# Thirty-two row dots moved from one phase to the other, and one product moved from VectorE to ScalarE, in a hybrid conv, attention and expert-retrieval block

## The chip, the cores and the metric

The kernel runs on one core of a Trainium2 chip. The metric is device microseconds per execution of that core. A TensorE matmul multiplies a stationary 128x128 tile by a moving tile; VectorE (DVE), ScalarE (ACT) and GpSimd (POOL) work on tiles of 128 partitions; SyncE (SP), ACT and POOL issue DMAs. Each engine runs its instructions in program order and waits on semaphores.

## The reference

One layer on 512 tokens of width 2048, in float32. The first half (modulated norm, one input projection, a convolution branch, an attention branch, an output projection) is untouched by the change. The second half, which the change touches, is a product-key retrieval over 16384 single-neuron experts: each token picks 8 x 16 = 128 experts, and its result is a gated sum over their rows of U and V.

```python
def peer(h, wq, k1, k2, u, v):
    ...
    experts = e1 * N_KEYS + e2                      # (tokens, 8, 16), 128 per token
    gates = jax.nn.softmax(best, axis=-1)
    def one_block(args):
        xb, eb, gb = args
        a = jnp.einsum("td,thkd->thk", xb, u[eb])   # row dots with U
        act = gb * jax.nn.gelu(a)
        return jnp.einsum("thk,thkd->td", act, v[eb])  # row steps with V
```

## The kernel before

The 512 tokens are split in three. **352 tokens** (TD) go the dense way: for all 16384 experts the activations are made on TensorE in 128 jobs over U, gated by a scattered gate matrix, and multiplied with V in 128 jobs. **128 tokens** (the last ones) and **32 extra tokens** (XT) go the sparse way: for each of their expert slots, GpSimd gathers a row of U or V for every partition by an indirect DMA (128 x 2048 float32), and VectorE multiplies it with the token ("dot", 128 of them; "dot_x" for the extra tokens, 32 of them) or adds it to the result ("v_step", 128 + 32).

**U jobs** (u_job, numbers 0 to 127). Job g needs tile g of U: SP loads it (load_raw, into one of four buffers, when job g-4 has ended), ACT copies it to a rounded tile (hi_raw, issued behind the Gelu of job g-3), VectorE subtracts to get the low part (lo_raw). TensorE then makes 16 x 3 matmuls of 352 columns. ACT applies Gelu and stores 176 KB to DRAM.

**Hots** (from job HOT = 69 on, 44 turns of 8 tokens, up to job 112). Beside the U job of a turn, VectorE builds one-hot tiles for 8 tokens (build_hots): an equality tile for the second key, one for the first key, and the first one times three bfloat16 pieces of the gate. TensorE multiplies them in 24 small matmuls; ACT copies the result (keep_hots) and stores it every fourth turn.

**End of U.** Jobs 113 to 127 have no hots. VectorE's order is lo_raw(n), then one or two dots, then lo_raw(n+1). The dots use a ring of three row buffers: GpSimd gathers row n only when dot n-3 is done. At jobs 121, 122 and 126 VectorE also weighs the first gate units (weigh, weigh_lo).

**V jobs** (v_job, numbers 0 to 127; tile 128 + q). The same chain of load, rounded copy and low part (v_lo), and besides a gate unit of 1.4 MB for every second job, loaded by SP (load_unit n waits for weigh_lo(n-1)). SP's queue is in order: load_unit(2) stands ahead of the load of tile 130, which V's third job needs. VectorE's first rows stand behind v_lo(5); a ring of four buffers holds them, and GpSimd gathers the first four at once when the last dot of U is done.

The rows are dealt out by counters: n_dot in U, n_row in V.

```python
            for n in range(HOT + N_HOTS, NKEY):
                if n > HOT + N_HOTS:
                    lo_raw(n)
                for m in range(2 if n % 2 else 1):
                    if n_dot < P:
                        dot(n_dot)
                    elif n_dot < P + XU:
                        dot_x(n_dot - P)
                    n_dot += 1
```

Of the kernel before, what the change touches and what calls it, by code (L numbers as in the profile page):

```python
# [9 lines left out]
ALU = mybir.AluOpType  # L10
# [46 lines left out]
NPRM = _n  # L57

LEAD, DMA_LEAD = 1, 16
XU = 16  # L60
N_CAND = 2 * TOPK + 6 * 8 + 8
SEL_G, TAB_G, SEL, TAB, HOT = 2, 10, 12, 60, 69
N_HOTS = TD // 8
# [35 lines left out]
def build(nc, x_d, xrow_d, c_d, pos_d, prm_d, wada_d, win_d, wqr_d, wval_d, whd_d, wout_d, wwq_d, keys_d, u_d, v_d, urow_d, vrow_d, out_d):  # L99
# [4 lines left out]
    with ExitStack() as ctx:  # L104
        def at(name, kb, shape, dt=F32):
            return nc.alloc_sbuf_tensor_at(name, shape, dt, offset=1152 + int(kb * 1024))
# [119 lines left out]
        x_keep = at("x_keep", 208, [P, KD, XT])  # L226
        x_rep = at("x_rep", 152, [P, KD, P // XT, XT])
        hot2 = at("hot2", 188, [P, 2, 4, P, 2], BF16)
        hot1 = [at(f"hot1{j}", 144 + 4 * j, [P, 2, 4, P, 2], BF16) for j in range(3)]
        gelu_s = [at(f"gelu_s{s}", 200 + 2 * s, [P, TD]) for s in range(2)]  # L230
        e1_c = at("e1_c", 204, [P, TD], BF16)
# [83 lines left out]
        gelu_ready = sem("gelu_ready")  # L315
        gelu_stored = [sem(f"gelu_stored{s}") for s in range(2)]
        hot_ready = [sem(f"hot_ready{s}") for s in range(2)]
        hot_used = [sem(f"hot_used{s}") for s in range(4)]
        g_copied = [sem(f"g_copied{s}") for s in range(2)]
        g_stored = [sem(f"g_stored{s}") for s in range(2)]  # L320
# [165 lines left out]
        def _(act):  # L486
# [335 lines left out]
            def gelu_job(u):  # L822
# [6 lines left out]
                act.dma_start(gelu_d[:, u:u + 1, :], gelu_s[u % 2][:].unsqueeze(1)).then_inc(gelu_stored[u % 2], 16)  # L829
                hi_raw(u + 3)  # L830

            def keep_hots(t):

                chunk, at_, cb = t // 4, 8 * (t % 4), t // 4 % 2
                if t % 4 == 0:
                    act.wait_ge(g_stored[cb], DMA_LEAD + 16 * (chunk // 2))
                for g in range(2):
                    act.wait_ge(hot_used[2 * (t % 2) + g], LEAD + t // 2 + 1)
                    act.activation(g_chunk[cb][:, :, at_ + 4 * g:at_ + 4 * g + 4], bank[2 + g][:].rearrange("p (t i) -> p i t", t=4),
                                   ACT.Copy).then_inc(g_copied[g], 1)  # L840
                if t % 4 == 3:
                    for g in range(2):
                        act.wait_ge(g_copied[g], LEAD + t + 1)
                    act.dma_start(gate_d[chunk], g_chunk[cb][:]).then_inc(g_stored[cb], 16)
# [10 lines left out]
            for u in range(2, NKEY):  # L855
                gelu_job(u)
                if u == TAB_G - 2:
                    act.wait_ge(gmax_ready, 1)
                    act.activation(expd_g[:], shifted_g[:], ACT.Exp).then_inc(gexp_ready, 1)
                if u == TAB - 1:  # L860
                    act.wait_ge(gmax_ready, 2)
                    act.activation(expd[:], shifted[:], ACT.Exp).then_inc(gexp_ready, 1)
                if HOT <= u < HOT + N_HOTS:
                    keep_hots(u - HOT)
                if u == 122:
                    act.wait_ge(dots_done, P)
                    act.activation(a_g[:], a_g[:], ACT.Gelu_apprx_tanh).then_inc(act_g_ready, 1)
                if u == 120:
                    weigh_hi(0)
                if u == 125:  # L870
                    weigh_hi(1)
# [45 lines left out]
        def _(dve):  # L917
# [551 lines left out]
            T_.step(dve.tensor_copy(gate_c[0][:], bank[4][:, 0:TD]))  # L1469
            T_.step(dve.tensor_tensor(gate_r[:], bank[4][:, 0:TD], gate_c[0][:], ALU.subtract))  # L1470
            T_.step(dve.tensor_copy(gate_c[1][:], gate_r[:]))
            T_.step(dve.tensor_tensor(gate_c[2][:], gate_r[:], gate_c[1][:], ALU.subtract))
            dve.sem_inc(tabt_used, 1)

            iotas = iota2[:].unsqueeze(1).broadcast_to([P, 4, P, 2])
# [4 lines left out]
            def build_hots(t):  # L1480

                u = t % 2
                dve.wait_ge(hot_used[2 * u + 1], LEAD + t // 2)
                tok = slice(8 * t, 8 * t + 8)
                one = T_.mark(dve.tensor_tensor(hot1[2][:, u], iotas, of_tokens(e1_c, tok), ALU.is_equal))
                dve.tensor_tensor(hot2[:, u], iotas, of_tokens(e2_c, tok), ALU.is_equal)
                T_.after(one)
                for j in range(3):
                    ins = dve.tensor_tensor(hot1[j][:, u], hot1[2][:, u], of_tokens(gate_c[j], tok), ALU.mult)
                ins.then_inc(hot_ready[u], 1)  # L1490

            def dot_x(n):
# [13 lines left out]
            for t in range(N_HOTS):  # L1506
                lo_raw(HOT + t + 1)
                if t < N_HOTS - 1:
                    build_hots(t + 1)
                for m in range(2 if t % 3 == 2 else 1):  # L1510
                    dot(n_dot)
                    n_dot += 1

            def weigh(n):
# [9 lines left out]
            for n in range(HOT + N_HOTS, NKEY):  # L1524
                if n > HOT + N_HOTS:
                    lo_raw(n)
                for m in range(2 if n % 2 else 1):
                    if n_dot < P:
                        dot(n_dot)
                    elif n_dot < P + XU:  # L1530
                        dot_x(n_dot - P)
                    n_dot += 1
                if n == 121:
                    weigh(0)
                elif n == 122:
                    weigh_lo(0)
                elif n == 126:
                    weigh(1)
# [49 lines left out]
                    v_step(n - (XT - XU))  # L1588

            for i in range(7):  # L1590
                if i == 6:
                    dve.wait_ge(act_x_ready, 1)
                    dve.wait_ge(y_x_set, 1)
                    T_.step(dve.tensor_tensor(gate_x[:], gate_x[:], a_x[:], ALU.mult))
                for r in range(16):
                    v_lo(6 + 16 * i + r)
                    for m in range(1 if r % 4 in (1, 2) else 2):
                        row(n_row)
                        n_row += 1
                    if r % 4 == 1:  # L1600
                        weigh(3 + 4 * i + r // 4)
                    elif r % 4 == 2:
                        weigh_lo(3 + 4 * i + r // 4)
                    if i == 0 and r == 8:
                        dve.wait_ge(x1_loaded, 32)
                    if r % 4 < 2:
                        add(2 * i + r // 8, r // 8, 2 * (r % 8 // 4) + r % 4)
                if i == 0:
                    dve.memset(y_x[:], 0.0).then_inc(y_x_set, 1)
            for e in range(10):  # L1610
                if e == 7:
                    close_half(1, 0, 14)
                v_lo(118 + e)
                if e < 4:
                    add(14, 0, e)
                if e == 1:
                    weigh(31)
                elif e == 2:
                    weigh_lo(31)
                for m in range(2 if e < 4 else 0):  # L1620
                    row(n_row)
                    n_row += 1
                if e == 3:
                    dve.wait_ge(y_g_steps, P + XT + 1)
                    dve.sem_inc(y_g_ready, 1)
# [3 lines left out]
        def _(pe):  # L1629
# [349 lines left out]
            for t in range(N_HOTS):  # L1979
                u_job(HOT + t)  # L1980
                u = t % 2
                pe.wait_ge(hot_ready[u], t // 2 + 1)
                for g in range(2):
                    pe.wait_ge(g_copied[g], LEAD + t)
                    for q in range(4):
# [110 lines left out]
```

## Time and profile before

| | |
|---|---|
| median of 3 runs | 3095.04 us (3094.26 to 3099.95) |
| the profiled execution's own time | 3093.42 us |
| its span, first to last instruction | 3091.6 us |
| TensorE busy | 2983.9 us, 97% of the span |
| VectorE busy | 2519.2 us, 81% |
| ScalarE busy | 1033.6 us, 33% |
| GpSimd busy | 781.7 us, 25% |
| DMA | 892.78 MB, mean 289 GB/s |

The share of an engine is an average over the whole kernel; what counts here is the second half, from about 1055 us on, where the U and V jobs lie. In the chain of work that ended last, TensorE holds 87% of the span. Times in the trace are microseconds from the span's start.

### The profile page before, as it was taken

How to read it: one execution, taken by the hardware profiler on the slowest of the kernel's cores; microseconds unless marked ns; L12 is line 12 of the kernel's file. 1: busy time of each engine (PE TensorE's matmuls, PEld its weight loads, DVE VectorE, ACT ScalarE, POOL GpSimd, SP SyncE). 2: the span in 40 equal slices, each digit the busy share in tenths (PEclk: the TensorE clock that was granted, in tenths of full speed). 3: DMA queues.
4: the chain of work that ended last, by engine and by line, in shares of the span. 5: the costliest groups of instructions: out<-in, count | busy, mean ns of one | idle time of the engine just before them, and what ended most of it. 6: DMA issues, size and time to landing. Idle time of an engine off the chain costs nothing.

```text
span 3091.6 us, 42071 instructions
## 1 busy us (share of the span) xinstructions
PE 2983.9 (97%) x17413; PEld 2756.3 (89%) x17413; DVE 2519.2 (81%) x3122; ACT 1033.6 (33%) x1094; POOL 781.7 (25%) x348
## 2 busy tenths in 40 slices
PE   6899989889899999999999999999999999999999
PEld 5786765467778999999999999998999999999999
DVE  7996968666763589989989898774989898989895
ACT  5323234431222333333333333332333334333331
POOL 0000000000120013333123333331455454545440
PEclk9999989999999999999999999999999999999999
DMA  9621233267644468888678988997999999999994
GB/s 382 277 95 68 89 111 121 96 254 296 264 164 163 147 251 337 324 336 321 246 290 339 356 346 336 385 377 304 387 394 389 391 394 389 393 390 393 389 393 173
DMA packets 182547, 892.78 MB, mean 289 GB/s; under 512 B 15713, under 2 KB 77281, under 8 KB 85857
## 3 DMA queue, kind: packets, MB, share of 16 engines
q1 hardware_dynamic: 111666, 490.25, 42.6%
q0 software_dynamic: 46080, 335.56, 26.6%
q10 hardware_dynamic: 24624, 64.45, 5.3%
q8 instruction: 130, 2.13, 0.3%
q14 instruction: 47, 0.39, 0.0%
HBM read 835.67 MB, written 54.53 MB: 288 GB/s over the span
## 4 chain that ended last, share of the span: by engine, by line
PE 87%; DVE 8%; ACT 3%; DMA 1%; issue 1%; POOL 0%; SPq 0%; ACTq 0%; DVEq 0%; POOLq 0%; PEldq 0%
PE bank L1953 11%; PE bank L1954 11%; PE bank L1955 11%; PE bank L2012 10%; PE bank L2014 10%; PE bank L2013 10%; PE bank L1637 3%; PE bank L1639 3%; PE bank L1638 3%; PE bank L1988 2%; PE bank L1889 2%; PE bank L1888 2%; DVE ada_w L969 2%; PE bank L1887 2%; DVE w_lo L936 1%
## 5 line engine op out<-in xcount | busy, mean ns | idle before, releaser
L471 POOL DMA_INDIRECT u_row<-u_rows,urow_i x128 | 287.5, 2246 | 823.5 <-DVE u_row L1406 559.0
L2012 PE MATMUL bank<-wt_hi,w_hi 128*128 128x352 f32 x1360 | 439.6, 323 | 7.3 <-DVE w_lo L923 4.7
L1953 PE MATMUL bank<-act_hi,w_hi 128*128 128x352 f32 x1376 | 446.6, 325 | 0.0
L1954 PE MATMUL bank<-act_lo,w_hi 128*128 128x352 f32 x1376 | 445.2, 324 | 0.0
L2013 PE MATMUL bank<-wt_lo,w_hi 128*128 128x352 f32 x1360 | 438.6, 323 | 0.0
L2014 PE MATMUL bank<-wt_hi,w_lo 128*128 128x352 f32 x1024 | 330.5, 323 | 0.0
L1955 PE MATMUL bank<-act_hi,w_lo 128*128 128x352 f32 x1024 | 330.0, 322 | 0.0
L1955 PE MATMUL bank<-act_hi,low 128*128 128x352 f32 x1024 | 330.0, 322 | 0.0
L2014 PE MATMUL bank<-wt_hi,low 128*128 128x352 f32 x1024 | 329.3, 322 | 0.0
L482 POOL DMA_INDIRECT u_row<-v_rows,urow_i x96 | 250.5, 2609 | 238.8 <-DVE y_g L1552 228.8
L1406 DVE SCALAR_TENSOR_TENSOR u_row<-u_row,h2t 128x2048 f32<-128x2048 f32 x128 | 288.6, 2284 | 14.9 <-DMA u_row<-u_rows,urow_i 14.9
L936 DVE TENSOR_TENSOR w_lo<-w_raw,w_hi 128x2048 fp32r<-128x2048 f32 (+1 forms) x63 | 139.9, 2221 | 172.0 <-ACT w_hi L492 167.9
L2012 PEld LDWEIGHTS bank<-wt_hi,w_hi 128*128 128x128 f32 x1360 | 256.6, 189 | 8.0 <-DVE w_lo L923 5.0
L1954 PEld LDWEIGHTS bank<-act_lo,w_hi 128*128 128x128 f32 x1376 | 258.8, 188 | 0.0
L1953 PEld LDWEIGHTS bank<-act_hi,w_hi 128*128 128x128 f32 x1376 | 258.3, 188 | 0.0
L2013 PEld LDWEIGHTS bank<-wt_lo,w_hi 128*128 128x128 f32 x1360 | 256.5, 189 | 0.0
L827 ACT ACTIVATE gelu_s<-bank 128x352 f32<-128x352 f32 x128 | 59.4, 464 | 585.1 <-PE bank L1955 581.2
L923 DVE TENSOR_TENSOR low<-w_raw,w_hi 128x2048 fp32r<-128x2048 f32 x86 | 196.7, 2287 | 68.8 <-ACT w_hi L801 68.7
L460 POOL TENSOR_TENSOR act_lo<-X,act_hi 128x512 fp32r<-128x512 f32 x16 | 28.6, 1799 | 842.7 <-ACT act_hi L516 842.7
L923 DVE TENSOR_TENSOR w_lo<-raw,w_hi 128x2048 fp32r<-128x2048 f32 x85 | 194.3, 2286 | 51.7 <-ACT w_hi L801 51.3
L1552 DVE SCALAR_TENSOR_TENSOR y_g<-u_row,gate_g,y_g 128x2048 f32<-128x2048 f32 x96 | 225.3, 2347 | 8.7 <-DMA u_row<-v_rows,urow_i 6.2
L801 ACT ACTIVATE w_hi<-raw 128x2048 fp32r<-128x2048 f32 x85 | 163.0, 1918 | 198.8 <-PE bank L2014 93.1
(348 smaller groups left out, 7200.2 us busy)
## 6 DMA issues: line engine op xcount, KB each, us to landing
ada_w<-wada SPq DMA_DIRECT2D x80, 1024.0 KB, 5.9
w_raw<-u SPq DMA_DIRECT2D x64, 1024.0 KB
raw<-u SPq DMA_DIRECT2D x64, 1024.0 KB
w_raw<-v SPq DMA_DIRECT2D x64, 1024.0 KB
raw<-v SPq DMA_DIRECT2D x64, 1024.0 KB
w_raw<-win SPq DMA_DIRECT2D x27, 1024.0 KB, 4.8
gelu_scratch<-gelu_s ACTq DMA_DIRECT2D x128, 176.0 KB
gate_scratch<-g_chunk ACTq DMA_DIRECT2D x11, 2048.0 KB, 12.1
```

Of the source, the lines that this page charges most:

```text
L471: pool.indirect_dma_start(u_row[n % 3][:], None, urow_d, bass.IndirectOffsetOnAxis(ap=col, axis=0)).then_inc(u_row_loaded[n % 3], 16)
L482: pool.indirect_dma_start(v_row[n % 4][:], None, table, bass.IndirectOffsetOnAxis(ap=col, axis=0)).then_inc(v_row_loaded[n % 4], 16)
L923: dve.tensor_tensor(in_tiles(low[g % 4]), in_tiles(raw[g % 4]), hi_of(g).bitcast(F32), ALU.subtract).then_inc(lo_done, 1)
L936: dve.tensor_tensor(w_lo[s][:, 0:width], w_raw[s][:, 0:width], w_hi[s][:, 0:width].bitcast(F32), ALU.subtract).then_inc(lo_done, 1)
L1406: dve.scalar_tensor_tensor(out=row, in0=row, scalar=1.0, in1=h2t, op0=ALU.mult, op1=ALU.mult, accum_out=a_g[:, n:n + 1]).then_inc(dots_don ...
L1552: dve.scalar_tensor_tensor(out=y[:], in0=v_row[n % 4][:], scalar=col, in1=y[:], op0=ALU.mult, op1=ALU.add).then_inc(y_g_steps, 1)
L1953: pe.matmul(out, wh[:, k, :], HD(k), start=(k == 0), stop=False)
L1954: pe.matmul(out, wh[:, k, :], LD(k), start=False, stop=False)
L1955: last = pe.matmul(out, wl[:, k, :], HD(k), start=False, stop=(k == KD - 1))
L2012: pe.matmul(o, wh[:, 8 * e + d, :], th, start=begin is not None and e == 0, stop=False)
L2013: pe.matmul(o, wh[:, 8 * e + d, :], tl, start=False, stop=False)
L2014: last = pe.matmul(o, wl[:, 8 * e + d, :], th, start=False, stop=bool(end) and e == 1)
```

## The change

Four things. XU, the number of extra tokens' dots done in U, goes from 16 to 32, so that V has no dots left. The dots in U are dealt faster: one and two in turn in the hots instead of one, one, two; and two per job after them instead of one and two in turn. In V 160 row steps are left of 176, dealt 11 to eight jobs instead of 12, and the extra tokens' gates are multiplied one group of 16 jobs earlier. Last, the equality tile has a buffer of its own (hot_eq), VectorE makes two gate products instead of three, and ScalarE makes the third, token by token, 8 instructions of 128 x 128 a turn with the gate as a per-partition scale (gate_hots); TensorE waits for both.

```diff
-XU = 16
+XU = 32
...
+            def gate_hots(t):
+
+                u = t % 2
+                act.wait_ge(hot_eq_ready[u], t // 2 + 1)
+                for n in range(8):
+                    ins = act.activation(hot1[2][:, u, n // 2, :, n % 2], hot_eq[:, u, n // 2, :, n % 2], ACT.Copy,
+                                         scale=gate_r[:, 8 * t + n:8 * t + n + 1])
+                ins.then_inc(hot_gated[u], 1)
...
+                if u == HOT - 1:
+                    act.wait_ge(tabt_used, 1)
+                    gate_hots(0)
                 if HOT <= u < HOT + N_HOTS:
                     keep_hots(u - HOT)
+                    if u < HOT + N_HOTS - 1:
+                        gate_hots(u - HOT + 1)
...
-                one = T_.mark(dve.tensor_tensor(hot1[2][:, u], iotas, of_tokens(e1_c, tok), ALU.is_equal))
+                dve.tensor_tensor(hot_eq[:, u], iotas, of_tokens(e1_c, tok), ALU.is_equal).then_inc(hot_eq_ready[u], 1)
                 dve.tensor_tensor(hot2[:, u], iotas, of_tokens(e2_c, tok), ALU.is_equal)
-                T_.after(one)
-                for j in range(3):
-                    ins = dve.tensor_tensor(hot1[j][:, u], hot1[2][:, u], of_tokens(gate_c[j], tok), ALU.mult)
+                dve.wait_ge(hot_eq_ready[u], t // 2 + 1)
+                for j in range(2):
+                    ins = dve.tensor_tensor(hot1[j][:, u], hot_eq[:, u], of_tokens(gate_c[j], tok), ALU.mult)
                 ins.then_inc(hot_ready[u], 1)
...
-                for m in range(2 if t % 3 == 2 else 1):
-                    dot(n_dot)
+                for m in range(1 + t % 2):
+                    if n_dot < P:
+                        dot(n_dot)
+                    else:
+                        dot_x(n_dot - P)
...
-                for m in range(2 if n % 2 else 1):
+                for m in range(2):
                     if n_dot < P:
                         dot(n_dot)
                     elif n_dot < P + XU:
...
-                if i == 6:
+                if i == 5:
                     dve.wait_ge(act_x_ready, 1)
...
-                    for m in range(1 if r % 4 in (1, 2) else 2):
+                    for m in range(1 if r % 8 in (1, 2, 3, 5, 6) else 2):
                         row(n_row)
...
-                for m in range(2 if e < 4 else 0):
+                for m in range(2 if e < 3 else 0):
                     row(n_row)
...
                 pe.wait_ge(hot_ready[u], t // 2 + 1)
+                pe.wait_ge(hot_gated[u], t // 2 + 1)
```

On VectorE, the end of U and the start of V stood like this: the low parts of tiles 126, 127, 128, 129 and 130 are the rows that write w_lo or low; the rows with a_x are dot_x; wt and wt_lo are weigh(1) and weigh_lo(1).

```order
L923 TENSOR_TENSOR w_lo1_66<-raw2_227,w_hi1_64 128x2048
L1500 SCALAR_TENSOR_TENSOR u_row1_186,a_x_178<-u_row1_186,h2x_189 128x2048
L1518 TENSOR_TENSOR wt_213<-wt_213,gate_l_214 128x1408
L923 TENSOR_TENSOR w_lo0_65<-raw3_228,w_hi0_63 128x2048
L1500 SCALAR_TENSOR_TENSOR u_row2_187,a_x_178<-u_row2_187,h2x_189 128x2048
L923 TENSOR_TENSOR low0_229<-w_raw1_62,hi_side_231 128x2048
L1522 TENSOR_TENSOR wt_lo1_210<-wt_213,wt_hi1_206 128x1408
L923 TENSOR_TENSOR low1_230<-w_raw0_61,w_hi1_64 128x2048
L1544 TENSOR_TENSOR gate_g_180<-gate_g_180,a_g_181 128x128
L923 TENSOR_TENSOR w_lo1_66<-raw2_227,w_hi0_63 128x2048
```

The same place with the change (its line numbers are higher by 16 to 19):

```order
L939 TENSOR_TENSOR w_lo1_66<-raw2_228,w_hi1_64 128x2048
L1516 SCALAR_TENSOR_TENSOR u_row0_185,a_x_178<-u_row0_185,h2x_189 128x2048
L1516 SCALAR_TENSOR_TENSOR u_row1_186,a_x_178<-u_row1_186,h2x_189 128x2048
L1537 TENSOR_TENSOR wt_214<-wt_214,gate_l_215 128x1408
L939 TENSOR_TENSOR w_lo0_65<-raw3_229,w_hi0_63 128x2048
L1516 SCALAR_TENSOR_TENSOR u_row2_187,a_x_178<-u_row2_187,h2x_189 128x2048
L1516 SCALAR_TENSOR_TENSOR u_row0_185,a_x_178<-u_row0_185,h2x_189 128x2048
L939 TENSOR_TENSOR low0_230<-w_raw1_62,hi_side_232 128x2048
L1541 TENSOR_TENSOR wt_lo1_211<-wt_214,wt_hi1_207 128x1408
L939 TENSOR_TENSOR low1_231<-w_raw0_61,w_hi1_64 128x2048
L1563 TENSOR_TENSOR gate_g_180<-gate_g_180,a_g_181 128x128
L939 TENSOR_TENSOR w_lo1_66<-raw2_228,w_hi0_63 128x2048
```

Tiles 126 and 127 are each followed by two dots instead of one, and so is every tile from 113 on; weigh_lo(1), on which SP's load_unit(2) waits, stands one dot further behind the low part of tile 127.

On ScalarE, one turn of the hots stood like this (Gelu, its store, the rounded copy of a tile, the two copies of the gate matrix):

```order
L827 ACTIVATE gelu_s1_197<-bank0 128x352
L829 DMA gelu_scratch<-gelu_s1_197 128x352
L801 ACTIVATE hi_side_231<-raw2_227 128x16x128
L839 ACTIVATE g_chunk0_183<-bank2 128x128x4
L839 ACTIVATE g_chunk0_183<-bank3 128x128x4
```

With the change:

```order
L829 ACTIVATE gelu_s0_197<-bank1 128x352
L831 DMA gelu_scratch<-gelu_s0_197 128x352
L803 ACTIVATE w_hi0_63<-raw3_229 128x2048
L850 ACTIVATE g_chunk1_184<-bank2 128x128x4
L850 ACTIVATE g_chunk1_184<-bank3 128x128x4
L855 DMA gate_scratch<-g_chunk1_184 128x4096
L839 ACTIVATE hot12_196<-hot_eq_193,gate_r_205 128x128 x8
```

The eight gate products of the next turn stand behind the copies of this one (this turn is one that also stores), ahead of the next Gelu.

## Rows read from the trace of the kernel before

**Rows 1.** Stretches: busy time of each engine, TensorE's clock, DMA share, rate.
```profile
core 0: us, PE busy (x) PEld busy (x) DVE busy (x) ACT busy (x) POOL busy (x), PEclk, DMA share, GB/s
1583.00:1977.00 394.00, 394.00 (x3119) 388.27 (x3119) 351.48 (x369) 144.59 (x173) 143.88 (x59) 1.00 0.89 343
1977.00:2080.00 103.00, 103.00 (x650) 103.00 (x648) 76.80 (x56) 32.15 (x29) 36.86 (x18) 1.00 1.01 400
2080.00:2090.00 10.00, 10.00 (x65) 10.00 (x64) 9.42 (x6) 6.47 (x6) 4.04 (x3) 1.00 0.40 138
2090.00:2112.00 22.00, 18.30 (x113) 17.72 (x112) 2.04 (x3) 2.72 (x3) 2.78 (x2) 1.00 1.02 397
2112.00:2140.00 28.00, 26.47 (x148) 26.47 (x149) 18.65 (x11) 12.64 (x14) 0.84 (x1) 0.88 0.48 187
...
2200.00:3050.00 850.00, 850.00 (x5345) 849.94 (x5344) 763.59 (x455) 293.23 (x244) 402.83 (x162) 1.00 0.98 385
```
**Rows 2.** What TensorE waited for, 1060 to 3092: total us, times, longest.
```profile
PE bank L2012 <- DVE w_lo L923: 4.7, 1, 4.7
PE bank L2012 <- DVE low L923: 2.4, 1, 2.4
```
**Rows 3.** DVE in order of time: start, us, instruction, [idle before it <- releaser].
```profile
2080.58 2.29 DVE L923 TENSOR_TENSOR w_lo<-raw,w_hi 128x2048 fp32r<-128x2048 f32 x1 [3.72 <-ACT w_hi L801]
2082.79 2.28 DVE L1500 SCALAR_TENSOR_TENSOR u_row<-u_row,h2x 128x2048 f32<-128x2048 f32 x1
...
2087.20 1.62 DVE L1522 TENSOR_TENSOR wt_lo<-wt,wt_hi 128x1408 fp32r<-128x1408 f32 x1
...
2111.19 2.29 DVE L923 TENSOR_TENSOR w_lo<-raw,w_hi 128x2048 fp32r<-128x2048 f32 x1 [19.96 <-ACT w_hi L801]
```
**Rows 4.** SP's queue in order of time, at the load of tile 130.
```profile
2089.70 11.88 SPq L405 DMA_DIRECT2D raw<-v  x2
```
**Rows 5.** GpSimd in order of time: first and last of V's first four gathers.
```profile
2085.35 2.75 POOL L482 DMA_INDIRECT u_row<-u_rows,urow_x  x1 [16.23 <-DVE u_row L1500]
...
2092.14 0.94 POOL L482 DMA_INDIRECT v_row<-u_rows,urow_x  x1 [0.30 <-issue]
```
**Rows 6.** ScalarE in order of time, the rounded copy of tile 130.
```profile
2109.17 1.91 ACT L801 ACTIVATE w_hi<-raw 128x2048 fp32r<-128x2048 f32 x1 [15.96 <-DMA raw<-v]
```
**Rows 7.** TensorE in order of time, V's third job after its wait.
```profile
2113.99 0.49 PE L2013 MATMUL bank<-wt_lo,w_hi 128*128 128x352 f32 x1
...
2119.57 0.39 PE L2014 MATMUL bank<-wt_hi,w_lo 128*128 128x352 f32 x1
```
**Rows 8.** The page's DMA queues: packets, bytes, share; GpSimd's gathers.
```profile
q0 software_dynamic: 46080, 335.56, 26.6%
```
**Rows 9.** DVE, 1977 to 2080, by shape: count, busy, mean ns, idle before.
```profile
L1500 DVE SCALAR_TENSOR_TENSOR u_row<-u_row,h2x 128x2048 f32<-128x2048 f32 x15 | 34.2, 2287 | 10.6 <-DMA u_row<-u_rows,urow_x 10.6
L1406 DVE SCALAR_TENSOR_TENSOR u_row<-u_row,h2t 128x2048 f32<-128x2048 f32 x5 | 11.4, 2288 | 12.0 <-DMA u_row<-u_rows,urow_i 12.0
```
**Rows 10.** The chain that ended last: the hots' matmuls of two turns.
```profile
1583.62 1.39 PE bank L1988 x24
1592.75 1.39 PE bank L1988 x24
```
**Rows 11.** DVE, 1583 to 1977, by shape: dots, gate products, equality tiles.
```profile
L1406 DVE SCALAR_TENSOR_TENSOR u_row<-u_row,h2t 128x2048 f32<-128x2048 f32 x59 | 133.6, 2283 | 3.6 <-DMA u_row<-u_rows,urow_i 3.6
...
L1489 DVE TENSOR_TENSOR hot<-hot,gate_c 128x1024 bf16<-128x1024 bf16 x126 | 79.3, 683 | 0.0
...
L1485 DVE TENSOR_TENSOR hot<-iota,e_c 128x1024 bf16<-128x1024 bf16 x42 | 28.9, 689 | 39.3 <-PE bank L1988 39.3
```
**Rows 12.** ScalarE's one instruction of 128 x 128: ns min/median/max.
```profile
L867 ACT ACTIVATE a_g<-a_g x1: 298/298/298, 2058.0 to 2058.0; 128x128 f32<-128x128 f32 x1
```
**Rows 13.** GpSimd in order of time, the gather of one row of U.
```profile
1996.80 2.75 POOL L471 DMA_INDIRECT u_row<-u_rows,urow_x  x1 [9.20 <-DVE u_row L1406]
```
**Rows 14.** DVE in order of time, the dot of that row, three dots later.
```profile
2008.45 2.29 DVE L1500 SCALAR_TENSOR_TENSOR u_row<-u_row,h2x 128x2048 f32<-128x2048 f32 x1 [2.46 <-DMA u_row<-u_rows,urow_x]
```

More of the change, by code:

```diff
@@ L228, in build @@
         hot2 = at("hot2", 188, [P, 2, 4, P, 2], BF16)
+        hot_eq = at("hot_eq", 192, [P, 2, 4, P, 2], BF16)
         hot1 = [at(f"hot1{j}", 144 + 4 * j, [P, 2, 4, P, 2], BF16) for j in range(3)]
@@ L317, in build @@
         hot_ready = [sem(f"hot_ready{s}") for s in range(2)]
+        hot_eq_ready, hot_gated = ([sem(f"{n}{s}") for s in range(2)] for n in ("hot_eq_ready", "hot_gated"))
         hot_used = [sem(f"hot_used{s}") for s in range(4)]
@@ L1471, in _ @@
             T_.step(dve.tensor_copy(gate_c[1][:], gate_r[:]))
-            T_.step(dve.tensor_tensor(gate_c[2][:], gate_r[:], gate_c[1][:], ALU.subtract))
+            T_.step(dve.tensor_tensor(gate_r[:], gate_r[:], gate_c[1][:], ALU.subtract))
             dve.sem_inc(tabt_used, 1)
```

## The prediction

> **What bounds the kernel now.** I read the stretches first, and look at TensorE's busy column against the length of each. In the hots (1583 to 1977) it is busy 394.00 of 394 us, at the end of U (1977 to 2080) 103.00 of 103, in most of V (2200 to 3050) 850.00 of 850 [rows 1]. The change adds and removes no matmul. So what it saves on VectorE or on the DMA queues in those stretches is worth nothing as long as TensorE stays covered, and can only cost. The second view, TensorE's waits from 1060 us on, says what there is to win: 4.7 us before V's third job (tile 130) and 2.4 us somewhat later [rows 2]. Behind the first of them TensorE runs at the lower of its two clock levels: 20 matmuls from 2113.99 to 2119.57 stand 0.29 us apart [rows 7], where the 650 of 103 us before stand 0.158 apart [rows 1], so 19 x 0.135 = 2.6 us more. 4.7 + 2.4 + 2.6 = 9.7 us is all that the second half can give.
>
> The third reading is the other columns of the stretches. In V the DMA share is 0.98 at 385 GB/s, in the hots 0.89 at 343, and at the end of U 1.01 at 400 GB/s [rows 1]: there the DMA engines have no time left already. VectorE is idle for 26 of those 103 us, and 10.6 + 12.0 = 22.6 us of it is waiting for gathered rows [rows 9]. The end of U is balanced on the DMA, with TensorE just covered.
>
> **The change part by part.**
>
> *Hots.* VectorE loses one product of 683 ns in each of 44 turns [rows 11], at most 30 us, and gets 8 dots more (66 instead of 58), 8 x 2.28 = 18 us [rows 11]. A turn is 9.13 us long [rows 10]; VectorE is busy 351 of 394 us and spends 39.3 us waiting for TensorE [rows 1, 11]. Cover: TensorE's 394 of 394. Worth zero. The 8 rows more are 8.4 MB (a row is 335.56 MB / 320 = 1.049 MB [rows 8]) in 394 us, 21 GB/s on 343; at 364 the DMA is still below its 400. Zero.
>
> *ScalarE's product.* The trace has no such instruction. Bounds: nothing beyond what hides it, and the nearest row, one ACTIVATE of 128 x 128, 298 ns [rows 12], which I take. 8 x 0.298 = 2.4 us a turn. ScalarE's load is 144.6 us in 394 [rows 1], 43 turns of 9.13 us, so 3.35 us a turn; with the product 5.7 of 9.13. Behind it in ScalarE's queue stands the Gelu of the next job, which isn't there before the turn is over, and the rounded copy of a tile three jobs ahead. Zero, with 3.4 us to spare.
>
> *V with 16 rows fewer.* 16.8 MB less for the DMA, 16 row operations less for VectorE, under a TensorE that is busy 850.00 of 850 us. Zero. The tail of the kernel has the same matmuls and the same output behind them.
>
> *The end of U, two dots in each job.* From the last turn of the hots to the low part of tile 127 the counters gave 143 - 121 = 22 dots; now they give 158 - 128 = 30. Per job of 9.13 - 1.39 = 7.7 us [rows 10] the DMA has a tile (1.05 MB), two rows (2.10) and a Gelu store (0.18): 3.33 MB, 432 GB/s, and two gate units of 1.4 MB on top. The stretch shows 400 at a full share [rows 1]. Eight rows more at 400 GB/s are 8 x 1.049 / 0.400 = 21.0 us by which the low part of tile 127 is later than 2080.58 [rows 3]. Lower bound: the dots fit into VectorE's 26 idle us, and nothing is late. Upper bound, by the ring of three row buffers: a gather issued at 1996.80 was used by a waiting dot at 2008.45, 11.65 us later [rows 13, 14]; with 0.35 us of issue and a dot of 2.2 us a ring turns in 14.2 us, so two rows take 9.5 us, 1.8 more than a job, 26 us over 15 jobs. I take 21.0, between them, since the share of 1.01 is the firmest row.
>
> *The way to tile 130.* This chain decides what a delay of the low part of tile 127 costs, because TensorE waits at its end already. At 2080.58 that low part begins; one dot ends U's dots at 2085.0 [rows 3]; GpSimd then gathers V's first four rows at once, 2085.35 to 2092 [rows 5]; weigh_lo(1) ends at 2088.8 [rows 3]; only then SP issues the gate unit and the load of tile 130, at 2089.70 [rows 4]; four rows, unit and tile share the DMA (share 1.02, 397 GB/s [rows 1]), ScalarE has the tile at 2109.17 [rows 6], and the low part begins at 2111.19 [rows 3]. TensorE starts when it ends. Nothing in this chain gets shorter: V's first four gathers are now rows of V, of the same size, and still behind the last dot. It gets one dot longer, 2.2 us, and that dot's row is gathered three dots earlier, too late by 11.65 + 0.35 - (2.2 + 1.6 + 2.3 + 2.2) = 3.7 us if nothing else waits in between, and by nothing if something does: 1.5 us. In the window from 2080 to 2090 the DMA is at 0.40 [rows 1]; that hole comes from the order of the queues and stays.
>
> **Sum.** 21.0 + 2.2 + 1.5 = 24.7 us later at tile 130, and everything after it moves along. 3093.42 + 24.7 = 3118.1 us, against the profiled execution's own time (the span is 1.8 us shorter); the median of the runs shown is 1.6 us above that execution, and I leave that out.
>
> The Trainium skill speaks against the size of it: its HBM Reference (section Specifications (TRN2)) says that a core that streams alone measures about 425 GB/s, bounded by its DMA engines. By that figure the end of U would move its 41.2 + 8.4 MB in 116.7 us, 13.7 us more than 103, and the sum would be 3111 us, an estimate. The trace's 400 GB/s at a full share does not reach that figure, but this stretch mixes small packets in.
>
> **Rivals.**
> - *Hidden.* The DMA takes the rows after all, VectorE's 26 idle us take 18 us of dots, and only the dot in the chain to tile 130 remains: 3093.4 + 2.2 = 3095.6. For it: the idle time, and a share of 0.40 right behind. Against it: VectorE's idle time is waiting for just these rows. It decides if the DMA moves 432 GB/s. 0.08.
> - *A higher rate.* The rate moves by 4% between V and the end of U (385 and 400) with the mix; if more gathered rows lift it by 4% again, to 416, 49.6 MB take 119.2 us, 16.2 more, and with 3.7 us of the chain the time is 3113. The page named above points this way. 0.10.
> - *Faster.* VectorE, freed of up to 30 us in the hots, enters the end of U ahead, the last dot falls earlier, GpSimd's four gathers are through before tile 130 is loaded, and TensorE's wait goes: 9.7 us at most, 3084. It decides if the low part of tile 130 is 4.7 us earlier. Against it: a low part can't run ahead of the rounded copy, which waits for TensorE's job three before, and two dots a job push the last dot back. 0.05.
> - *ScalarE too slow.* If a product of 128 x 128 with a per-partition scale takes over (9.13 - 3.35) / 8 = 0.72 us, TensorE waits in every turn: at 0.8 us 44 x 8 x 0.08 = 28 us on top of the forecast, 3146. Against it: 298 ns. 0.05.
>
> **How the numbers follow.** The forecast has 0.72. Its own upper end is the ring's 26 us with 2.2 + 3.7 us and one more fall of TensorE's clock (2.6): 34.5, some 3128; a second and third fall make 3133. The lower end, 3101, lies between the hidden case and the higher rate: about a third of the 21 us. 3101 to 3133 leaves out the hidden, the faster and the ScalarE case, 0.18. Slower by over 0.2% (6 us, about what a measurement of this kernel can tell from no change): 0.72 + 0.10 + 0.05 = 0.87; within it 0.08; faster 0.05.
>
> **What would show it.** In the changed profile TensorE should wait for the low parts of U's tiles in the jobs from 114 on, some 15 to 20 us in sum, in pieces of 1 to 4 us, with a DMA share of about 1.0 at 400 GB/s and VectorE waiting for rows; the wait before tile 130 should grow from 4.7 to some 10 us; the hots and V should stay at a full TensorE, V at a DMA share near 0.94. ScalarE's products should take about 0.3 us, and no wait on them should be seen. I am wrong if the end of U moves over 420 GB/s with TensorE busy throughout, if tile 130 is ready earlier than now counted from tile 127, or if TensorE's row for the hots' matmuls shows idle time before it.

## The result, and the profile after

The changed kernel takes 3134.3 us in the median (3133.12 to 3138.63), the kernel before 3094.65 (3092.92 to 3099.95): ratio 1.0127, 95% interval 1.0114 to 1.0139, 39.7 us slower. The forecast was 24.7 us, the upper end of the range 3133. The profiled execution of the changed kernel took 3138.63 us (span 3136.8), 45.2 us more than that of the kernel before; it is the slowest of those timed, and 2.4 us of its distance are there before the first turn of the hots, ahead of all that the change touches. Below, "later" is always against the kernel before's profile, at the same job.

The changed kernel's stretches, in the columns of [rows 1]; the hots now end at 1984, and the low part of tile 127, where I let the end of U stop, begins at 2116.1.

```profile
core 0: us, PE busy (x) PEld busy (x) DVE busy (x) ACT busy (x) POOL busy (x), PEclk, DMA share, GB/s
1583.00:1984.00 401.00, 397.50 (x3132) 390.63 (x3132) 344.53 (x342) 247.31 (x520) 156.42 (x66) 1.00 0.91 356
1984.00:2116.10 132.10, 114.13 (x683) 111.58 (x680) 94.99 (x72) 35.17 (x31) 52.27 (x27) 0.96 0.98 389
2128.00:2150.00 22.00, 15.84 (x98) 15.27 (x96) 2.58 (x3) 3.50 (x3) 2.54 (x2) 0.92 1.03 407
2200.00:3090.00 890.00, 882.87 (x5528) 881.42 (x5529) 761.04 (x449) 312.67 (x259) 377.04 (x153) 1.00 0.94 364
2000.00:2020.00 20.00, 14.90 (x80) 14.88 (x80) 16.41 (x13) 4.76 (x4) 9.05 (x4) 0.83 0.85 335
2010.00:2018.00 8.00, 8.00 (x52) 8.00 (x51) 7.61 (x6) 2.26 (x2) 3.37 (x2) 1.00 0.62 209
2100.00:2115.00 15.00, 11.44 (x72) 11.15 (x70) 7.31 (x8) 4.17 (x3) 3.83 (x3) 1.00 1.01 422
2115.00:2120.00 5.00, 1.52 (x5) 1.53 (x6) 5.00 (x3) 3.29 (x3) 0.00 (x0) 0.57 0.20 79
```

TensorE is no longer full in the hots, at the end of U or in V: 3.5 us are missing in the hots, 18 at the end of U, 7 in V. Its waits from 1060 us on, the view of [rows 2] (L1972 are U's jobs, L2008 the hots' matmuls, L2032 V's jobs):

```profile
PE bank L1972 <- DVE w_lo L939: 14.6, 5, 7.0
PE bank L2032 <- DVE low L939: 7.2, 4, 2.9
PE bank L2032 <- DVE w_lo L939: 6.4, 1, 6.4
PE bank L1972 <- DVE low L939: 5.7, 3, 3.1
PE bank L2008 <- issue: 3.4, 7, 0.8
```

Before, 4.7 and 2.4 us stood here. The wait before tile 130 is the 6.4. New are 14.6 + 5.7 = 20.3 us for low parts of U's tiles, in jobs 115 to 127. VectorE, in order of time, shows what they are made of:

```profile
2000.56 2.29 DVE L1516 SCALAR_TENSOR_TENSOR u_row<-u_row,h2x 128x2048 f32<-128x2048 f32 x1 [9.14 <-DMA u_row<-u_rows,urow_x]
...
2002.78 2.29 DVE L939 TENSOR_TENSOR w_lo<-raw,w_hi 128x2048 fp32r<-128x2048 f32 x1
...
2116.13 2.29 DVE L939 TENSOR_TENSOR w_lo<-raw,w_hi 128x2048 fp32r<-128x2048 f32 x1
2118.34 2.29 DVE L1516 SCALAR_TENSOR_TENSOR u_row<-u_row,h2x 128x2048 f32<-128x2048 f32 x1
...
2120.55 2.29 DVE L1516 SCALAR_TENSOR_TENSOR u_row<-u_row,h2x 128x2048 f32<-128x2048 f32 x1
...
2124.96 1.62 DVE L1541 TENSOR_TENSOR wt_lo<-wt,wt_hi 128x1408 fp32r<-128x1408 f32 x1
...
2148.41 2.29 DVE L939 TENSOR_TENSOR w_lo<-raw,w_hi 128x2048 fp32r<-128x2048 f32 x1 [19.42 <-ACT w_hi L803]
```

At 2000.56 a dot has waited 9.14 us for its gathered row, and the low part of a tile, queued behind it, starts only at 2002.78: that is how a late row becomes a wait of TensorE. The low part of tile 127 begins at 2116.13, that of tile 130 at 2148.41; [rows 3] have 2080.58 and 2111.19.

The DMA of the end of U, each time up to the low part of tile 127: first of the kernel before (1977 to 2080.5), then of the changed one (1984 to 2116.1); q0 are GpSimd's gathers.

```profile
DMA packets 9826, 41.45 MB, mean 400 GB/s; under 512 B 803, under 2 KB 5283, under 8 KB 5539
q0 software_dynamic: 2732, 19.86, 46.7%
```

```profile
DMA packets 11326, 51.45 MB, mean 389 GB/s; under 512 B 976, under 2 KB 5584, under 8 KB 5840
q0 software_dynamic: 4005, 29.14, 54.7%
```

10.0 MB more, 9.3 of them rows, at a rate that has fallen by 3%. At 400 GB/s the 51.45 MB would take 128.6 us, 25.1 more than 103.5; the rate of 389 adds the other 3.5.

### The profile page after: what moved, and what is told of

Its sections match the earlier page's. It is cut to its first block, busy times and chain, and to the rows that moved or that the text cites. A ratio compares the mean times of both kernels' runs of the same rounds, so it can differ in the third digit from the quotient of the medians.

```text
span 3136.8 us, 42380 instructions
## 1 busy us (share of the span) xinstructions
PE 3000.2 (96%) x17413; PEld 2764.1 (88%) x17413; DVE 2495.0 (80%) x3078; ACT 1142.7 (36%) x1446; POOL 769.0 (25%) x348
## 4 chain that ended last, share of the span: by engine, by line
PE 78%; DVE 10%; DMA 7%; ACT 3%; issue 1%; POOL 0%; SPq 0%; ACTq 0%; DVEq 0%; POOLq 0%; PEldq 0%
PE bank L1972 9%; PE bank L1973 9%; PE bank L1974 9%; PE bank L2032 9%; PE bank L2034 9%; PE bank L2033 9%; PE bank L1656 3%; PE bank L1657 3%; PE bank L1658 3%; DMA u_row<-u_rows,urow_x 3%; DMA w_raw<-v 2%; PE bank L2008 2%; PE bank L1908 2%; PE bank L1907 2%; DVE ada_w L985 2%; PE bank L1906 2%
## 5 line engine op out<-in xcount | busy, mean ns | idle before, releaser
L1972 PE MATMUL bank<-act_hi,w_hi 128*128 128x352 f32 x1376 | 449.7, 327 | 16.0 <-DVE w_lo L939 12.8
L2032 PE MATMUL bank<-wt_hi,w_hi 128*128 128x352 f32 x1360 | 440.7, 324 | 14.0 <-DVE low L939 7.2
L484 POOL DMA_INDIRECT u_row<-v_rows,urow_i x96 | 240.9, 2510 | 336.7 <-DVE y_g L1571 314.5
L1972 PEld LDWEIGHTS bank<-act_hi,w_hi 128*128 128x128 f32 x1376 | 260.3, 189 | 17.8 <-DVE w_lo L939 14.0
L2032 PEld LDWEIGHTS bank<-wt_hi,w_hi 128*128 128x128 f32 x1360 | 256.9, 189 | 15.8 <-DVE low L939 8.8
```

The costliest lines, as they stand in the source:

```text
L484: pool.indirect_dma_start(v_row[n % 4][:], None, table, bass.IndirectOffsetOnAxis(ap=col, axis=0)).then_inc(v_row_loaded[n % 4], 16)
L1972: pe.matmul(out, wh[:, k, :], HD(k), start=(k == 0), stop=False)
L2032: pe.matmul(o, wh[:, 8 * e + d, :], th, start=begin is not None and e == 0, stop=False)
```

## The experiments

Theory A, the prediction's: the end of U has no DMA time for more rows, and bytes alone make it late. Rival B: it isn't bytes, but the ring of three buffers (a gather may start only three dots ahead). Rival C: the end of U is late from its entry on, where VectorE comes behind out of the hots. Rival D: ScalarE's product costs TensorE time in the hots. Medians of the kernel before in brackets are those of the same session.

**ScalarE's product alone** (the changed kernel with the dealing of before):

```diff
-XU = 32
+XU = 16
...
-                for m in range(1 + t % 2):
+                for m in range(2 if t % 3 == 2 else 1):
...
-                for m in range(2):
+                for m in range(2 if n % 2 else 1):
```

> The kernel before with ScalarE's product alone; rows dealt as before. If ScalarE's product only makes TensorE wait in the hots, as the changed profile shows (job ends 4.75 us later over 44 turns), the time is 3098 to 3101 us, with all the additional waiting before the hots' matmuls. If it also pushes the rounded copies of the tiles back and so takes part in the waits at the end of U, it is 3105 us or more, with waits of U jobs 114 on. If the hots' waits need the heavier gathers to appear, it is 3094 to 3096.

Measured: 3097.58 us (3096.19), ratio 1.0003 [0.9994, 1.0013]. The time falls between two of the expectation's branches. In the profile the hots' matmuls wait 0.5 us, once. The product by itself costs nothing that can be told.

**The rows alone** (the changed kernel with all three products on VectorE):

```diff
-                for j in range(2):
-                    ins = dve.tensor_tensor(hot1[j][:, u], hot_eq[:, u], of_tokens(gate_c[j], tok), ALU.mult)
+                for j in range(3):
+                    ins = dve.tensor_tensor(hot1[j][:, u], hot1[2][:, u], of_tokens(gate_c[j], tok), ALU.mult)
...
-                pe.wait_ge(hot_gated[u], t // 2 + 1)
```

> The changed kernel with all three gate products back on VectorE; rows dealt as changed. If the dealing of the rows alone makes the end of U late: 3127 to 3131 us, the changed time less the 4.75 us of the hots. If ScalarE's product is a condition of it: below 3115.

Measured: 3131.94 us (3096.19), ratio 1.0121 [1.0104, 1.0139]. TensorE's waits for U's low parts, in its profile:

```profile
PE bank L1967 <- DVE w_lo L934: 15.8, 4, 6.0
...
PE bank L1967 <- DVE low L934: 4.5, 3, 2.3
```

20.3 us in sum again, and no row for the hots' matmuls. The time is 0.9 us above the first branch. So the loss is mainly the rows' and not the product's. But the product isn't neutral either: without it VectorE waits 23.5 us for rows in the hots (up to 1977) instead of 2.4, TensorE leaves the hots on time, and job 114 then ends 8.9 us late. What the product costs in the hots it saves at the entry of the end of U.

**Two dots per job at the end of U, nothing else** (the kernel before, XU = 16; the hots get fewer dots, so that the count is the same):

```diff
-                for m in range(2 if t % 3 == 2 else 1):
+                for m in range(2 if t % 7 == 6 else 1):
...
-                for m in range(2 if n % 2 else 1):
+                for m in range(2):
```

> The kernel before, XU still 16 and V untouched; 8 dots fewer in the hots (50 instead of 58) and two dots in every job after them. Only the dealing at the end of U is as changed. If two dots a job are more than the gathers and the DMA carry: 3118 to 3128 us, with TensorE waiting some 18 to 22 us for low parts of tiles 114 to 127. If it is the number of dots in U or the shorter row list of V that costs: 3094 to 3098.

Measured: 3121.41 us (3096.19), ratio 1.0077 [1.0054, 1.01], 25.2 us slower. This is the prediction's mechanism without hots that are heavier, without the product and without a changed V, and it costs about what the sum gave (24.7). Its end of U:

```profile
1983.00:2113.00 130.00, 115.73 (x689) 113.98 (x687) 96.65 (x72) 37.09 (x34) 49.87 (x26) 0.95 0.98 390
```

Counted from the start of the hots, the low part of tile 127 is 23.5 us later and the end of its job 21.6; TensorE waits 14.2 us for low parts of U, where 18 to 22 were expected, and 8.6 us before tile 130. Up to the low part of tile 127 this dealing has seven dots more than before, not eight, so that the prediction's formula gives 7 x 1.049 / 0.400 = 18.4 us for 23.5.

**A ring of four** (the changed kernel; from dot 132 on the rows lie in four buffers):

```diff
-                if n >= 3:
+                if n >= R4 + 4:
+                    pool.wait_ge(dots_done, n - 3)
...
+                elif n >= 3:
                     pool.wait_ge(dots_done, n - 2)
```

> The changed kernel with four row buffers instead of three from dot 132 on (the fourth is V's own fourth, free after the hots). If the DMA's bytes are the limit (3.33 MB a job at 400 GB/s), a fourth buffer gives nothing: 3129 to 3136 us, waits at the end of U as in the changed kernel. If it is the turn of three buffers (14.2 us or more for three rows), it takes most of the waits away: 3105 to 3118.

Measured: 3132.63 us (3096.19), ratio 1.0114 [1.0098, 1.0131]. Waits for low parts of U are still there, 14.5 us in three pieces up to 7.4, and the stretch up to its low part of tile 127 is full:

```profile
1982.00:2108.00 126.00, 114.18 (x693) 113.24 (x690) 95.16 (x72) 32.61 (x30) 54.31 (x27) 0.93 1.01 403
```

Rival B falls as the cause: gathers that may start a dot earlier share the same DMA time. But a part is the ring's. From job 113 to the end of job 127 this profile loses 20.3 us, the changed kernel's 28.4; 1.2 of it come back in the hots, 1.9 at tile 130 and 1.0 in V, and against the kernel before of its own session the median is 36.4 us higher (39.7 for the changed kernel), which the two intervals don't tell apart.

**Half rows at the end of U** (the changed kernel; from dot 130 on a gather brings 1024 of a row's 2048 elements, so the extra tokens' result isn't computed):

```diff
+                if n < 130:
...
+                else:
+                    pool.indirect_dma_start(u_row[n % 3][:, 0:D // 2], None, urow_d.rearrange("n (h d) -> (n h) d", h=2), bass.IndirectOffsetOnAxis(ap=col, axis=0)).then_inc(
```

> The changed kernel, but the gathers for dots 130 to 159 bring half a row (1024 columns, of other experts' rows; the other half of the buffer keeps older data), so the result of the extra tokens is not the reference's. Same instructions and waits, 0.52 instead of 1.05 MB a gather, 2.3 MB a job. If the bytes make the end of U late: its waits go, 3098 to 3106 us, the hots' waits and the one before tile 130 staying. If a gather costs the same whatever it brings (issue, ring, order on VectorE): 3122 us or more.

Measured: 3113.12 us (3098.48), ratio 1.0048 [1.0031, 1.0065]. Instructions, their conditions and the ring are the same, only bytes are fewer. The time lies between the two branches of the expectation. Its end of U, up to the low part of tile 127:

```profile
1984.00:2094.00 110.00, 108.61 (x685) 107.16 (x685) 93.26 (x70) 35.92 (x32) 54.33 (x27) 1.00 0.92 327
```

and TensorE's waits:

```profile
PE bank L2036 <- DVE w_lo L943: 8.5, 1, 8.5
PE bank L2036 <- DVE low L943: 5.8, 4, 2.4
PE bank L2012 <- issue: 3.2, 8, 0.6
PE bank L1976 <- DVE low L943: 0.9, 2, 0.7
PE bank L1976 <- DVE w_lo L943: 0.6, 3, 0.2
```

U's waits fall from 20.3 to 1.5 us, at a DMA share of 0.92, and from job 113 to the end of job 127 only 3.5 us are lost, where the changed kernel loses 28.4. Theory A holds: bytes make the end of U late. What is left are the other terms: 4.6 us in the hots, 3.8 before tile 130 (a wait of 8.5 against 4.7), 5.3 from there on, in V. The expectation had left V's share out.

**The rows in the hots instead** (the changed kernel; the end of U has its one and two dots in turn again, the hots get 73 dots):

```diff
-                for m in range(1 + t % 2):
+                for m in range(2 if t % 3 else 1):
...
-                for m in range(2):
+                for m in range(2 if n % 2 else 1):
```

> The changed kernel (all 32 extra dots in U, product on ScalarE), but the 15 jobs after the hots deal one and two dots in turn as before, and the hots take the seven dots more (two in two of three turns, 73). If only the load of the last jobs costs: 3095 to 3103 us, no waits of U jobs 114 to 127 over 1 us; the hots then ask for 383 GB/s, still under 400. If 16 more dots in U cost wherever they lie: 3115 us or more.

Measured: 3122.62 us (3098.48), ratio 1.0078 [1.0061, 1.0095]. The time falls into the second branch; I had held that the hots' DMA has room for all of it. The last 77 us of its hots,

```profile
1900.00:1977.00 77.00, 73.40 (x580) 72.05 (x577) 66.06 (x65) 48.48 (x99) 29.27 (x14) 1.00 0.97 382
```

have little room: up to 1977 VectorE waits 37.1 us for the 128 tokens' rows and 7.5 for the extra tokens', 10.9 of it in these 77 us (2.4 in all in the changed kernel), the hots end 8.7 us late, and a single wait of 8.6 us follows at 2004. From then on the end of U holds its distance (20.9 us at the end of job 114 and at job 127): at one and two dots in turn it loses nothing.

**A smooth entry** (the changed kernel; the last four turns of the hots have 2, 2, 2 and 0 dots, since before tile 114 four dots stand in a row):

```diff
-                for m in range(1 + t % 2):
+                for m in range((2, 2, 2, 0)[t - 40] if t >= 40 else 1 + t % 2):
```

> The changed kernel with the same number of dots in the hots, but none in the last turn (turns 40 to 43: 2, 2, 2, 0 instead of 1, 2, 1, 2), so that two dots and not four stand in a row ahead of the low part of tile 114. If the first wait of the end of U (5.1 us at job 115 and 2.4 us of lower clock, 7.5 us in sum) comes from that row of four: 3124 to 3129 us. If the bytes only fall due later: 3131 to 3136.

Measured: 3138.02 us (3098.48), ratio 1.0125 [1.0107, 1.0142]. No help: the time is above both branches, and job 115 still ends 6.6 us late against job 113. The first wait isn't made by the four dots.

**V dealt as before** (the changed kernel; V's rows go 12 to eight jobs and run out earlier):

```diff
-                    for m in range(1 if r % 8 in (1, 2, 3, 5, 6) else 2):
-                        row(n_row)
+                    for m in range(1 if r % 4 in (1, 2) else 2):
+                        if n_row < P + XT:
+                            row(n_row)
...
-                for m in range(2 if e < 3 else 0):
-                    row(n_row)
-                    n_row += 1
```

> The changed kernel with V's row steps dealt as before, 12 to eight jobs, so that the 160 rows are used up in the seventh group of 16 jobs and not at the end. If TensorE's new waits in V (4.3 us and 1.8 us of lower clock in the changed profile, where VectorE reaches a gate unit before it has landed) come from the thinner dealing: they go until the rows run out, 3127 to 3132 us. If they come from the rows' kind or from something ahead of V: 3133 to 3138.

Measured: 3133.1 us (3097.93), ratio 1.0114 [1.0094, 1.0134]. In its profile TensorE doesn't wait between 2206 and 3095 and VectorE waits for no gate unit there, where the changed kernel has 4.3 and 24.5 us. The other profiles agree: from tile 130 to the end V loses 4.0 to 9.0 us in the six kernels with the thinner dealing and 0.5 to 1.3 in the four with the dealing of before. So the thinner dealing makes V's stalls. The time doesn't show the gain: at 3133.1 it lies in the second branch, and against the kernel before of its own session it is 35.2 us slower (39.7 for the changed kernel), which the two intervals don't tell apart.

**Three causes out at once** (the changed kernel with half rows, the products on VectorE and V dealt as before; the extra tokens' result isn't computed):

```diff
-                pool.indirect_dma_start(u_row[n % 3][:], None, urow_d,
+                pool.indirect_dma_start(u_row[n % 3][:, 0:D // 2], None, urow_d.rearrange("n (h d) -> (n h) d", h=2),
...
-                for j in range(2):
+                for j in range(3):
...
-                    for m in range(1 if r % 8 in (1, 2, 3, 5, 6) else 2):
+                    for m in range(1 if r % 4 in (1, 2) else 2):
```

> The changed kernel with three causes taken out together: half rows for dots 130 to 159 (the extra tokens' result is not the reference's), all gate products on VectorE, V's row steps dealt as before. If the loss is the sum of bytes at the end of U, waits in the hots and waits in V: 5 to 9 us over the kernel before, what is left being VectorE's one dot more and the longer wait before tile 130 (8.5 instead of 4.7 us), with no TensorE wait in the hots and none in V from 2205 us to the last 40 us. If there is another cause: 12 us or more, as with the half rows alone (14.6).

Measured: 3109.17 us (3095.41), ratio 1.0051 [1.0038, 1.0065], 13.8 us slower, no better than half rows alone. The expectation missed, because it took the terms as a sum. TensorE's waits:

```profile
PE bank L2028 <- DVE w_lo L938: 8.4, 1, 8.4
PE bank L1969 <- DVE w_lo L938: 5.7, 4, 3.0
PE bank L2028 <- DVE low L938: 2.9, 1, 2.9
PE bank L1969 <- DVE low L938: 1.2, 2, 0.6
```

Nothing is lost in the hots now and 0.7 us in V, but 5.7 + 1.2 = 6.9 us stand at the end of U, where half rows alone left 1.5, and they stand at its first jobs. V's dealing lies behind these, so the third product on VectorE makes the difference: it gives back at the entry what the hots had gained. That is rival C; it is real, but the smaller cause.

**Tile 130 first** (the kernel before; SP loads tile 130 ahead of the gate unit):

```diff
-            for g in range(NKEY - 1, NKEY + 2):
+            for g in range(NKEY - 1, NKEY + 3):
                 load_raw(g)
             load_unit(2)
```

> The kernel before, with SP's load of tile 130 ahead of gate unit 2 instead of behind it. If the wait before tile 130 comes from that order (the load stands 4.6 us behind its own condition): the 4.7 us of waiting and the 2.6 us of lower clock go, 3087 to 3090 us. If the four gathers hold the tile up in any order: 3092 to 3097.

Measured: 3093.81 us (3098.48), ratio 0.9985 [0.9974, 0.9997]. That is the second branch's time. In its profile (3087.35 us, the fastest of its executions) the 4.7 us of [rows 2] are gone, but 2.4 us come up one tile later: tile 131, issued at 2096.88, lands at 2110.7, beside the unit, four gathers and a load of 2 MB.

**The start of V in order** (the same, and gate unit 3 earlier, V's first gathers held until V's first job is over, the 2 MB load behind the copy of tile 131):

```diff
-                if q == 8:
+                if q == 6:
                     load_unit(3)
...
+            pool.wait_ge(pe_jobs, J_V + 1)
...
-            act.dma_start(acc_o[:, 0:8, :], x1_d[:, 0:8, :]).then_inc(x1_loaded, 16)
...
+                    act.dma_start(acc_o[:, 0:8, :], x1_d[:, 0:8, :]).then_inc(x1_loaded, 16)
```

> The kernel before, rows dealt as before, with the start of V cleared: tile 130 ahead of gate unit 2 in SP's queue, gate unit 3 two tiles earlier, V's first four gathers held until V's first job has ended, and the load of the residual (2 MB) one tile later in ScalarE's queue. If TensorE's waits at the start of V come from what is in flight together there: they go, 9.7 us at most, 3084 to 3088 us against 3094 to 3098 of the kernel before. If the same bytes only come late elsewhere: within 3 us of the kernel before.

Measured: 3088.38 us (3097.93), ratio 0.9968 [0.9956, 0.998]: 9.5 us faster than the kernel before, and the lowest median here. TensorE's waits in its profile:

```profile
PE bank L2013 <- ACT stage L883: 3.8, 2, 2.3
PE bank L2013 <- ACT gelu_s L829: 0.6, 1, 0.6
```

Both of [rows 2] are gone; what remains is a wait for ScalarE's copies in V. In this execution (3092.42 us, the slowest of its session) V's first ten jobs gain 10.4 us, and 6.0 are lost again later, around these waits. The second half of the kernel before had about the 9.7 us to give that the prediction read from it. Which of the four moves gives how much was not taken apart.

## Why the prediction was right in its direction and short by 15 us

Right: slower, by the DMA at the end of U, through dots that wait for rows ahead of the low parts. That the DMA has no time left at the end of U was the step that decided, and half rows show it. What was off is the size of four terms, counted in the profiled execution:

| term | predicted, us | measured, us |
|---|---|---|
| hots | 0 | 4.75 |
| end of U, to the low part of tile 127 | 21.0 | 28.4 |
| from there to tile 130 | 3.7 | 1.7 |
| V, from there on | 0 | 8.0 |

Together 42.8 for 24.7; with the 2.4 us that are there before the hots this is the whole 45.2. The median is lower by 4.3 us than that execution. So three steps failed, one sized too small and two put at zero, and the way to tile 130 was sized too large. Of the signs, TensorE's waits for low parts of U came out at 20.3 us in pieces of up to 7.0 (15 to 20, up to 4, forecast), and one spoke against the working: the row for the hots' matmuls has idle time, 3.4 us.

*The end of U (the step that failed first: "Eight rows more at 400 GB/s are 21.0 us").* The low part of tile 127 is 35.55 us later, 7.15 of which job 113 brings along: 28.4 us for 21.0. The upper bound I gave was 26. Two things were left out. The stretch carries 10.0 MB more, not 8.4: 8.9 rows instead of 8, and 0.7 MB of tiles, units and stores that had been moved ahead of it, or behind, before. That is 25.1 us at 400 GB/s. And the rate isn't a constant of the stretch: the mean is 389, which makes the other 3.5. It is not lower throughout. From 2100 to 2115, where TensorE already stands still for 3.6 us, the DMA moves 422 GB/s at a full share. The largest hole is 2010 to 2018, 0.62 and 209 GB/s: tile loads wait for a job that has ended, job 115 starts 5.1 us late and ends at 2015.3, and SP issues no load of a tile between 2000.05 and then. With a fourth row buffer the stretch has no such loss in the mean (1.01 and 403 GB/s) and costs 20.3 us, so that the ring of three has a part in it. The fall behind 2115 (0.20) corresponds to the hole that [rows 1] have from 2080 to 2090, and lies behind U's last rows. TensorE's clock falls three times behind waits; jobs 115, 120 and 127 take 2.3, 1.7 and 2.0 us more than before by it, and the sum had none.

The two dots a job by themselves cost 25.2 us in a kernel that was otherwise the one before. That this is near 24.7 is luck in part: for its seven rows more the formula gives 18.4 us and the low part of tile 127 is 23.5 later, while the way from there to tile 130 takes 2.0 us more and not 3.7. The Trainium skill's 425 GB/s for a core that streams alone (HBM Reference, section Specifications (TRN2)) would have made the forecast 3111, an estimate. The trace doesn't agree for a mean over the stretch: 400 at a full share before, 389 after, with 422 only in a part of it; and the mean is what the term needs.

*The hots ("Zero, with 3.4 us to spare").* ScalarE, in order of time, in one turn:

```profile
1968.59 1.92 ACT L803 ACTIVATE hi_side<-w_raw 128x2048 fp32r<-128x2048 f32 x1 [3.73 <-DMA w_raw<-u]
1970.41 1.06 ACT L850 ACTIVATE g_chunk<-bank 128x512 f32<-128x512 f32 x2
1971.36 2.48 ACT L839 ACTIVATE hot<-hot_eq,gate_r 128x128 bf16<-128x128 bf16 x8
1973.70 0.45 ACT L829 ACTIVATE gelu_s<-bank 128x352 f32<-128x352 f32 x1
```

and TensorE's matmuls of this turn:

```profile
1973.94 1.54 PE L2008 MATMUL bank<-hot,hot 128*128 128x128 bf16 x24 [0.46 <-issue]
```

The price was right, 2.48 us for eight, 0.31 each. The slack wasn't: the products stand behind the rounded copy, which waits 3.73 us for a tile, and end at 1973.84; TensorE stands still for 0.46 us and starts at 1973.94. I had added up ScalarE's work and left out that its queue waits for a landing. Nine of the 44 turns, nearly every fourth one, take 9.24 to 10.03 instead of 9.13 us. The 2 MB store of the gate matrix comes every fourth turn too; whether it is what holds the tile up was not tested. It takes both, the product and the heavier DMA: with the product alone the hots lose 0.9 us, with the rows alone none. Rival "ScalarE too slow" was the right place with the wrong reason.

*Tile 130.* The wait grew from 4.7 to 6.4 us, not to some 10: the chain kept its order, and the dots there didn't wait.

*V ("Zero").* Less work isn't less waiting here. There are 32 gate units for V's 128 jobs, one for every fourth and not for every second as stated above. Their gate halves in the changed kernel, and VectorE around one of them:

```profile
DMA to landing us min/median/max: 8.8/13.9/23.9
```

```profile
2618.40 2.35 DVE L1571 SCALAR_TENSOR_TENSOR y_g<-v_row,gate_g,y_g 128x2048 f32<-128x2048 f32 x1
2625.62 1.63 DVE L1537 TENSOR_TENSOR wt<-wt,gate_l 128x1408 f32<-128x1408 f32 x1 [4.88 <-DMA gate_l<-gate_scratch]
...
2631.61 2.29 DVE L939 TENSOR_TENSOR low<-w_raw,w_hi 128x2048 fp32r<-128x2048 f32 x1 [3.49 <-ACT w_hi L803]
```

VectorE waits 24.5 us for units there, in four pieces. In three of them it comes to the weigh 12.5 to 15.3 us after the unit's load was issued (before the change it weighs 17 to 20.5 us after), and the unit isn't there yet. In the one shown, which costs TensorE most, VectorE comes 19 us after, no earlier than before, and the unit lands late, 23.9 us after its issue; it waits 4.88 us, and the low part behind it is late. V dealt as before has none of these waits, and its units land earlier too, after 8.5 to 21.0 us with a median of 10.9. So the thinner dealing brings VectorE earlier and the units later; why the units come later isn't shown. The cover that I named, a busy TensorE, was no cover against an in-order engine that arrives ahead of its input.

Left open: how the first wait of the end of U (5.1 us ahead of job 115 and 2.3 of lower clock in it, 7.5 by the end of that job) divides between the rows in the hots, the last 2 MB gate store and the pace of two dots. It was 10.6 us with the rows in the hots, 8.9 with the rows alone, 6.6 with the smooth entry, 5.2 a job later with two dots alone, and 0 with half rows. The last gate store was not moved by itself.

## What to carry to other kernels

Where the DMA has no time left, work that is moved into that stretch costs at least its bytes over the rate, whatever engine looks idle. If loads are released by the engine that the lateness stalls, the stream can get holes where its jobs end late (here one of 8 us at a share of 0.62), so the bytes over the old rate are a lower end. Count slack on an in-order engine to the moment its last input lands, not as busy time against the period. Giving an engine less work can make it wait earlier in its queue, since the work that was taken away had hidden a part of a load's latency. And what had looked like a small stall at a phase's start (here 9.7 us) was the better thing to change.

## What the runs showed that I had not expected

- The DMA share was not the limit that a mean suggests: in the hots 0.91 at 356 GB/s already has waits in it, and 0.97 at 382 over 77 us makes VectorE wait 10.9 us for rows.
- A load of a gate unit took from 8.8 to 23.9 us to land in one execution, and the load of tile 131 beside a unit 13.8 us, 2096.88 to 2110.7, in the kernel with tile 130 first.
- ScalarE's product of 128 x 128 with a scale per partition takes 0.31 us back to back (8 in 2.48 us); its row by lines has a mean of 434 ns, which is not its price in a group.
- Behind five of its waits, of 2.6 to 7.0 us, TensorE ran at the lower of its two clock levels in the changed kernel's second half; its matmuls stood some 0.29 instead of 0.16 us apart for 3.5 to 5.5 us, and each such fall cost 1.7 to 2.5 us more, some 10 in sum. Before there was one, of 2.6 us.
